# Placing the last two experts' rows with a 0/1 matrix on TensorE instead of through the table in memory

## The chip, the cores and the metric

One core of a Trainium2 chip runs the whole program. The metric is the device time of one execution in microseconds, as the median of three runs.

## The reference, cut to what matters

A sequence of 512 tokens of width 1024 goes through two blocks in f32. The first block ends with a mixture of 32 experts; each token goes to two of them. The second block begins with a final norm of the first, a norm of its own, and a product with `w_in_a_2`.

```python
expert = g_idx[:, None] * EXPERTS_PER_GROUP + top_i          # two experts per token
...
yb = (jax.nn.silu(x_blk @ w1[e]) * (x_blk @ w3[e])) @ w2[e]   # per expert, its own tokens
yb = yb * buf_w[:, None]
out = jnp.zeros((n_tok + 1, d)).at[buf_tok].add(yb)[:n_tok]   # every token sums its two rows
...
x = x + out
x = rms_norm(x, norm_final_g)                                 # "x3" before, "x4" after it
h = rmsnorm(x, ln_a); b, c, u, z = split(h @ w_in_a, 4)       # next: chunk c0 of this product
```

## The kernel before

Five engines run their own programs and meet at semaphores. The tokens lie in `x_rows`, four tiles `t` of 128 tokens by 1024 columns. PSUM has eight banks of 128 x 512 f32.

**The expert stage.** Each expert has 64 places ("slots") for its tokens; experts with more would use an overflow loop whose length `over_n` is read from memory at run time, and which doesn't run with these inputs. Per expert `e` TensorE turns the gathered rows, multiplies them with `w1` and `w3` (`hidden`, L1175: 16 matmuls, two at a time, one for output partitions 0 to 63 and one for 64 to 127), ScalarE makes the silu (L1648), VectorE the product with the other half (L2252), TensorE turns it (`turn_gated`, L1183), ScalarE copies it (L1651), and `down` (L1192) multiplies with `w2`: 8 matmuls, again two at a time, columns 0 to 511 of the result into partitions 0 to 63 of one bank and columns 512 to 1023 into partitions 64 to 127 of the same bank. An f32 matmul stands in the trace as two records, so `hidden` has 32 and `down` 16. VectorE weighs the result (`weigh`, L2255) into `y_sb`, and GpSimd scatters it by an indirect DMA into the table `y_dram` (L793), which has two half rows of 512 for each token and each of its two choices. The expert weights, 6 MB each, come over SP's queue into three slots, and SP waits for the expert three back before it loads a slot again (L653).

**Between the experts and the next product.** SP loads the raw chunk `c0` (two halves of 1 MB) once `hidden` of expert 30 is done, and `u0` after `hidden` of expert 31 (L606). When all rows are stored, SP loads eight pieces `y_back[t]` of `y_dram` (L685), for each tile one per choice, and the two gain rows `g_fin` and `g_a_row` (L688, L689). Every chunk needs a rounded high part, made by ScalarE (`high_half`, L1462), and a low part, made by VectorE (`low_half`, L2319), before TensorE multiplies in three passes (L874 to L876). VectorE then goes through a list written by hand:

- `add_back(t)` (L2325, L2326): two adds of 128 x 1024 into `x_rows`
- `scale_final(t)` (L2333): times `g_fin`
- `normalise_x4(t)` (L2339 to L2348): three small operations, a wait for ScalarE's root (L1441), a reciprocal, one 128 x 1024 product; ScalarE makes the two sums of squares for it (L1430)
- `low_x4(t)` (L2357): the low part of the turned tile; TensorE turns it (`turn_x4`, L1270) and ScalarE makes its high part (L1697)

in the order add 0, add 1, scale 0, scale 1, normalise 0, normalise 1, add 2, low 0, low 1, scale 2, add 3, normalise 2, scale 3, normalise 3, low 2, low 3. TensorE turns tiles 0 and 1, multiplies `c0` with the first 256 tokens (turning tiles 2 and 3 on the way) and then with the other 256. `spin` (L864) is dummy matmuls of 256 columns ahead of it.

Of the kernel before, what the change touches and what calls it, by code (L numbers as in the profile page):

```python
# [35 lines left out]
ALU = mybir.AluOpType  # L36
# [161 lines left out]
def second_plan():  # L198

    first = [(("x4_t", t, b), "dve") for t in range(NT) for b in range(2)]  # L200
# [7 lines left out]
    opened = closed[0:4] + [("c", j) for j in range(4)] + closed[4:8] + closed[12:]  # L208
# [87 lines left out]
def build(nc, a, out):  # L296
# [7 lines left out]
    with ctx:  # L304
# [112 lines left out]
        over_slot = w_slot[2]  # L417
        xg = [E[:, 0:512], E[:, 512:1024], B0[:, 1536:2048]]
        y_sb = [E[:, 1024:1536], E[:, 1536:2048]]
        xgT = [f3(B0, (4, 2, SLOTS), 512 * b) for b in range(2)]  # L420
# [58 lines left out]
        g_fin, g_a_row = B0[:, 0:D], B0[:, D:2 * D]  # L479
# [117 lines left out]
        def _(sp):  # L597
# [10 lines left out]
            for c in range(first_chunks):  # L608
# [4 lines left out]
                if c == 0:  # L613
                    sp.dma_start(w_gates, w_cols(w_in, 3584, 8)).then_inc(sem("w_gates_loaded"), 16)
                if c == 1:
# [48 lines left out]
            for n, c in enumerate(("c0", "u0")):  # L664
                sp.wait_ge(h_done, EXPERTS - 1 + n)
                for h in range(2):
                    load_half(2 * chunk_no[c] + h)
# [13 lines left out]
            sp.wait_ge(sem("pe_left_experts"), 1)  # L681
            for t in range(NT):
# [4 lines left out]
                if t == 1:  # L687
                    sp.dma_start(g_fin, a["norm_final_g"].partition_broadcast(P)).then_inc(sem("g_fin_loaded"), 16)  # L688
                    sp.dma_start(g_a_row, a["ln_a_2"][0].partition_broadcast(P)).then_inc(sem("g_a_row_loaded"), 16)  # L689

# [14 lines left out]
        def _(pool):  # L705
            more = sem("more_loaded2")
            pool.memset(convT[:, :, 0:CONV1 - 1], 0.0).then_inc(sem("pads_zero"), 1)
            pool.memset(mv_rows[:, :, :, P:P + 1], 1.0).then_inc(sem("pads_zero"), 1)
            loads = [(gate_b[32 * g:32 * g + HEADS, g:g + 1], a["ml_gate_b"][0, g].rearrange("(h o) -> h o", o=1))
# [106 lines left out]

            with pool.Fori(0, 4) as i:
                for n in range(6):
                    step_rows(6 * i + n, n)
            for e in range(24, EXPERTS):  # L820
                step_rows(e, e)
            for b in range(2):
                pool.wait_ge(sem(f"y_stored{b}"), 16 * EXPERTS // 2)

            n = pool.value_load(over_n, min_val=0, max_val=OVER)
            with pool.If(n > 0):
                with pool.Fori(1, OVER + 1) as k:
# [5 lines left out]
                                            y_sb[0], None, bounds_check=4 * SEQ - 1, oob_is_err=False)\  # L833
# [15 lines left out]
        def _(pe):  # L849
# [376 lines left out]

            spin(bank[0], 8)
# [28 lines left out]
            pe.nop().then_inc(sem("pe_left_experts"), 1)  # L1256


            done[0] = 0

            def turn_x4(t):

                for b in range(2):
                    o = fill(V, "x4_t", t, b)
                    if t == 0 and b == 0:
                        pe.wait_ge(sem("x3_ready"), 1)
                        spin(o, 9)
# [9 lines left out]
            spin(outs[0], 4)  # L1277
# [136 lines left out]
        def _(act):  # L1414
# [92 lines left out]
            for i in range(16 + 3):  # L1507
                if i < 16 and i % 4 == 0:
                    high_parts(("mk", "mv", "mo", "wo0")[i // 4])
                if i < 16:  # L1510
# [13 lines left out]
                    elif i >= 12:  # L1524
                        o = filled(U["proj", i])
                        act.activation(moT[:, i - 12, :], o[:, :], ACT.Copy).then_inc(done, 1)
# [126 lines left out]
            def pair(i, first=False):  # L1653
                for b in range(2):
                    e = 2 * i + b
                    act.wait_ge(h_done, e + 1)
                    if not first:
                        act.wait_ge(sem("g_ready"), e - 1)
                    silu(b).then_inc(sem("silu_e_ready"), 1)
                    act.wait_ge(g_turned, e + 1)  # L1660
                    if not first:
                        act.wait_ge(sem("y_done"), e - 1)
                    gated_cols(b).then_inc(sem("gT_ready"), 1)

            pair(0, True)
            with act.Fori(1, EXPERTS // 2) as i:
                pair(i)
            act.wait_ge(sem("y_done"), EXPERTS)
            wait_emptied(act, U["table",])
# [10 lines left out]
            high_parts("c0", "u0")  # L1680
            act.activation(root[:, 79:80], ms[:, 79:80], ACT.Sqrt)

            def square_x3(t):

                act.wait_ge(sem("x3_ready"), t + 1)
                sums(x_rows, t, 16 + t)

            def square_x3g(t):

                act.wait_ge(sem("x3g_ready"), t + 1)  # L1690
                sums_of(x3g[t], 20 + t)
# [7 lines left out]

            square_x3(0)  # L1700
            square_x3(1)
            for t in range(2):
                square_x3g(t)
                roots(16 + 2 * t, 18 + 2 * t)
            high_x4(0)
            high_x4(1)
            square_x3(2)
# [6 lines left out]
            high_x4(3)  # L1714
            for t in range(NT):
# [110 lines left out]
        def _(dve):  # L1826
# [419 lines left out]

            def rows_cols(b):
# [45 lines left out]
            pair(EXPERTS // 2 - 1, False, True)  # L2293
            step_weigh(EXPERTS // 2 - 1, 1)
            n = dve.value_load(over_n, min_val=0, max_val=OVER)
            with dve.If(n > 0):
                with dve.Fori(0, OVER) as k:
# [5 lines left out]
                    weigh(0, k + EXPERTS).then_inc(sem("y_ready"), 1)  # L2303
                    dve.wait_ge(sem("ov_stored"), 16 * k + 16)

            def low_half(name, h):

                g = 2 * chunk_no[name] + h  # L2310
                dve.wait_ge(w_high_ready, g - 1)
                lo, hi = quarter(g, False), quarter(g, True)
                if name in chunk_gain:
                    gain = chunk_gain[name]
# [252 lines left out]
```

## Time and profile before

| what | us |
|---|---|
| median of 3 runs | 1489.03 (1488.64 to 1490.09) |
| the profiled execution | 1489.01 |
| its span, first to last instruction | 1487.2 |
| TensorE busy | 1347.6 (91%) |
| VectorE busy | 536.3 (36%) |
| ScalarE busy | 414.2 (28%) |
| GpSimd busy | 391.8 (26%) |
| mean granted TensorE clock, share of full speed | 0.964 |

The expert stage lies between about 545 and 998 us; the stretch from 980 to 1043 us is where the change works. Busy time is an average over stages: only a wait that ends last in its stage sets the time.

### The profile page before, as it was taken

To read this page: it belongs to the slowest core of one execution; us is meant where nothing else is said; L and a number is where in the kernel's file an instruction comes from. 1 tells how busy PE (TensorE), PEld (TensorE's weight loads), DVE (VectorE), ACT (ScalarE), POOL (GpSimd) and SP (SyncE) were. 2 spreads that over 40 slices of the span, in tenths; PEclk is the share of its full clock that TensorE was granted. 3 is DMA by queue.
4 is the path that set the end of the run, shared out by engine and by line. 5 is a ranking of instruction groups with operands and counts; after the bars stand their busy time and mean duration, and the time that the engine had idled before them with its cause. 6 is when DMAs were issued, how large, how long until landed. Compare 5 with 4: busy or idle time off the path is not lost. (4 is left out here: it accounts for less than half of the span.)

```text
span 1487.2 us, 16780 instructions
## 1 busy us (share of the span) xinstructions
PE 1347.6 (91%) x6344; PEld 897.6 (60%) x6344; DVE 536.3 (36%) x1074; ACT 414.2 (28%) x810; POOL 391.8 (26%) x372
## 2 busy tenths in 40 slices
PE   7999998999999899988878888876999999999799
PEld 6777776898768733323323223225888887788467
DVE  3649857430242511111111111117321414563753
ACT  5333356163331100000000000014323224343641
POOL 7553223168320111111111111100444450000321
PEclk9999998999999699999999999998999999999999
DMA  7221131244205879999999999983232322222000
GB/s 209 75 97 57 58 113 64 85 164 142 85 5 213 357 297 391 418 423 422 421 423 422 422 424 421 423 339 142 85 114 85 106 93 85 85 85 85 29 22 36
DMA packets 72368, 298.27 MB, mean 201 GB/s; under 512 B 10168, under 2 KB 10216, under 8 KB 51568
## 3 DMA queue, kind: packets, MB, share of 16 engines
q1 hardware_dynamic: 64848, 282.80, 48.5%
q0 software_dynamic: 7456, 14.59, 3.0%
q8 instruction: 43, 0.70, 0.2%
q14 instruction: 21, 0.17, 0.0%
HBM read 293.16 MB, written 12.58 MB: 206 GB/s over the span
## 5 line engine op out<-in xcount | busy, mean ns | idle before, releaser
L747 POOL TENSOR_TENSOR ring_rounded<-ring,ring_rounded 128x512 fp32r<-128x512 f32 x192 | 254.1, 1362 | 348.0 <-ACT ring_rounded L1462 348.0
L874 PE MATMUL bank<-HT_rounded,ring_rounded 128*128 128x512 f32 (+1 forms) x576 | 221.2, 384 | 4.6 <-DVE ring_rounded L2357 3.5
L875 PE MATMUL bank<-ring_rounded 128*128 128x512 f32 (+1 forms) x576 | 217.6, 378 | 0.0
L876 PE MATMUL bank<-HT_rounded,ring_rounded 128*128 128x512 f32 (+1 forms) x576 | 217.6, 378 | 0.0
L1175 PE MATMUL bank<-ring,B 128*64 128x512 f32 x704 | 172.2, 639 | 43.4 <-DMA ring<-in_w 42.4
L1175 PEld LDWEIGHTS bank<-ring,B 128*64 128x64 f32 x704 | 52.6, 145 | 146.8 <-issue 106.4
L2249 DVE TENSOR_TENSOR B<-bank,small 128x512 f32<-128x512 f32 x32 | 22.1, 691 | 327.6 <-PE bank L1165 327.6
L876 PE MATMUL bank<-ring_rounded 128*128 128x512 f32 x352 | 137.7, 391 | 0.0
L1462 ACT ACTIVATE ring_rounded<-ring 128x2048 fp32r<-128x2048 f32 x54 | 102.7, 1915 | 106.1 <-DMA ring<-in_w_in_a 46.7
L874 PEld LDWEIGHTS bank<-HT_rounded,ring_rounded 128*128 128x128 f32 x576 | 108.5, 188 | 31.6 <-issue 6.2
L875 PEld LDWEIGHTS bank<-ring_rounded 128*128 128x128 f32 x576 | 108.5, 188 | 20.5 <-issue 1.0
L876 PEld LDWEIGHTS bank<-HT_rounded,ring_rounded 128*128 128x128 f32 x576 | 108.4, 188 | 20.3
L1648 ACT ACTIVATE B<-bank 64x512 f32<-64x512 f32 x32 | 18.9, 589 | 328.3 <-PE bank L1175 328.3
L874 PE MATMUL bank<-ring_rounded,XN_rounded 128*128 128x512 f32 x256 | 101.6, 397 | 1.7 <-DVE X L2409 1.5
L875 PE MATMUL bank<-ring_rounded,XN_rounded 128*128 128x512 f32 x256 | 99.7, 390 | 0.0
L1175 PE MATMUL bank<-XN,B 128*64 128x512 f32 x160 | 81.7, 665 | 18.1 <-DMA HT<-in_w 18.0
L844 POOL TENSOR_TENSOR HT<-HT,small 128x1024 f32<-128x1024 f32 (+1 forms) x16 | 26.9, 1684 | 209.8 <-DVE small L2529 209.8
L1175 PE MATMUL bank<-HT,B 128*64 128x512 f32 x160 | 81.8, 665 | 0.0
L782 POOL COPY ints<-ints 128x1 int32 x48 | 9.2, 191 | 267.1 <-DVE E L2255 265.0
L1192 PE MATMUL bank<-A,B 128*64 128x512 f32 x336 | 76.7, 598 | 0.5 <-ACT B L1651 0.5
L876 PEld LDWEIGHTS bank<-ring_rounded 128*128 128x128 f32 x352 | 66.5, 189 | 14.2
L874 PE MATMUL bank<-ring_rounded,HT_rounded 128*128 128x512 f32 x160 | 65.3, 408 | 3.5 <-DVE ring_rounded L2402 3.5
(382 smaller groups left out, 1994.5 us busy)
## 6 DMA issues: line engine op xcount, KB each, us to landing
ring<-in_w SPq DMA_DIRECT2D x88, 1024.0 KB, 30.3
A<-in_w SPq DMA_DIRECT2D x21, 2048.0 KB, 28.7
ring<-in_w SPq DMA_DIRECT2D x11, 2048.0 KB, 28.8
XN<-in_w SPq DMA_DIRECT2D x20, 1024.0 KB, 29.1
HT<-in_w SPq DMA_DIRECT2D x20, 1024.0 KB, 32.3
ring<-in_w_in_a SPq DMA_DIRECT2D x16, 1024.0 KB, 5.1
ring<-in_w_in SPq DMA_DIRECT2D x14, 1024.0 KB, 7.3
ring<-in_w_in_b SPq DMA_DIRECT2D x8, 1024.0 KB, 5.3
```

What stands on the lines that cost most here:

```text
L747: last = pool.tensor_tensor(r32(lo), lo, r32_read(quarter(g, True)[:, k, :]), ALU.subtract)
L782: pool.tensor_copy(dst, src).then_inc(written, 1)
L844: pool.tensor_tensor(S, S, rz[:, c + 4:c + 8].unsqueeze(2).to_broadcast([P, 4, n]), ALU.mult)\
L874: pe.matmul(o, r32(a_hi), r32(b_hi), start=first, stop=False)
L875: pe.matmul(o, r32(a_hi), r32(b_lo), start=False, stop=False)
L876: return pe.matmul(o, r32(a_lo), r32(b_hi), start=False, stop=last)
L1175: last = pe.matmul(bank[2 + b][64 * j:64 * j + 64, :], xgT[b][:, k, hf, :], w, start=(n == 0), stop=(n == 7), skip_group_check=True)
L1192: last = pe.matmul(bank[6 + b][64 * hf:64 * hf + 64, :], gT[b][:, k, :], w[:, k, 512 * hf:512 * hf + 512], start=(k == 0), stop=(k == 3), ...
L1462: last = act.activation(r32(hi), raw, ACT.Copy)
L1648: return act.activation(sil[b][SLOTS:P, :], bank[2 + b][0:SLOTS, :], ACT.Silu)
L2249: return dve.tensor_tensor(xgT[b], bank[b][:, :].rearrange("p (k h s) -> p k h s", k=4, h=2), g, ALU.mult)
```

## The change

- The kernel zeroes all of `y_dram` early: GpSimd clears a 128 x 512 tile `y_over`, and SP writes it out in four DMAs of 1 MB behind the fourth weight chunk. GpSimd waits for them before the experts, ScalarE before it writes `moT`, which shares the tile's memory.
- Experts 0 to 29 are scattered as before. For 30 and 31 `down_last(j, n)` puts columns 0 to 511 into bank 6 and 512 to 1023 into bank 7, both at partitions 64·j to 64·j+63, so that the two banks hold 128 slots of both experts.
- VectorE weighs bank 6 and ScalarE bank 7 into `y_last` (128 x 1024). VectorE makes, between `weigh` of expert 29 and the gate of 31, a 0/1 matrix `last_oh` (128 slots by 512 tokens).
- For each tile, `last_rows(t)` multiplies `last_oh` with `y_last` into two banks, and VectorE adds them to `x_rows` (`add_last`). For tile 1 TensorE also adds both `y_back` pieces through the identity, and VectorE's `add_back(1)` is gone.
- SP loads `y_back` once rows 0 to 29 are stored and `down_last(0)` is done, and `u0` behind it. `g_fin` and `g_a_row` move to `A1`.
- ScalarE makes `c0`'s high halves during expert 31, the first one ahead of silu 31; VectorE makes both low halves before the last weighing. `u0`'s high halves go behind `high_x4(1)` and `high_x4(3)`.
- VectorE's list is: add 0, last 0, scale 0, last 1, scale 1, normalise 0, add 2, normalise 1, low 0, last 2, last 3, low 1, scale 2, add 3, normalise 2, scale 3, normalise 3, low 2, low 3. The spins are 4 and 3 matmuls instead of 9 and 4.

```diff
+            def down_last(j, n):
+                pe.wait_ge(sem("gT_ready"), PAIR + j + 1)
+                pe.wait_ge(we_loaded[n % 3][2], 16 * ((PAIR + j) // 3 + 1))
+                pe.wait_ge(sem("y_ready"), PAIR)
...
+                for k in range(4):
+                    for hf in range(2):
+                        last = pe.matmul(bank[6 + hf][64 * j:64 * j + 64, :], gT[n % 2][:, k, :],
+                                         w[:, k, 512 * hf:512 * hf + 512], start=(k == 0), stop=(k == 3),
+                                         skip_group_check=True)
...
-            step_down(4, 6)
+            down_last(0, 6)
             step(4, 7)
-            step_down(4, 7)
+            down_last(1, 7)
             pe.wait_ge(sem("y_ready"), EXPERTS)
+            pe.wait_ge(sem("y_last_ready"), 1)
...
+            def last_rows(t):
+                for b in range(2):
+                    o = fill(V, "last", t, b)[:, :]
+                    cs = slice(512 * b, 512 * b + 512)
+                    if t == 1:
+                        pe.wait_ge(sem("y_back1"), 32)
+                        for c in range(2):
+                            pe.matmul(o, ident, y_back[t][:, c, cs], start=(c == 0), stop=False)
+                    pe.matmul(o, last_oh[:, P * t:P * t + P], y_last[:, cs], start=(t != 1), stop=True)\
+                      .then_inc(bank_filled, 1)
...
+            last_rows(0)
+            last_rows(1)
             turn_x4(0)
+            last_rows(2)
+            last_rows(3)
             turn_x4(1)
...
+            one(PAIR // 2, 0)
+            high_half("c0", 0)
+            one(PAIR // 2, 1)
+            high_half("c0", 1)
             act.wait_ge(sem("y_done"), EXPERTS)
+            act.wait_ge(sem("y_stored1"), 16 * PAIR // 2)
+            act.wait_ge(sem("last_oh_ready"), 1)
+            act.activation(y_last[:, 512:1024], bank[7][:, :], ACT.Copy, scale=last_scale)\
+               .then_inc(sem("y_last_ready"), 1)
...
+            step_gate(PAIR // 2, 1)
+            for h in range(2):
+                low_half("c0", h)
+            dve.wait_ge(sem("y_done"), EXPERTS)
...
+            dve.tensor_scalar(y_last[:, 0:512], bank[6][:, :], last_scale, None, ALU.mult).then_inc(sem("y_ready"), 2)
```

## Rows read from the trace of the kernel before

**Rows 1.** Windows (columns: stretch, length, busy time of each engine, PEclk, DMA share, GB/s)

```profile
1042.50:1487.00 444.50, 425.75 (x2096) 340.30 (x2096) 186.48 (x342) 158.90 (x339) 110.09 (x80) 1.00 0.23 76
960.00:975.00 15.00, 11.49 (x56) 4.30 (x56) 2.13 (x3) 0.90 (x2) 1.01 (x1) 1.00 1.01 425
```

**Rows 2.** Timeline of TensorE, last experts and first product (start, us, what)

```profile
980.94 3.65 PE L1192 MATMUL bank<-A,B 128*64 128x512 f32 x16 [0.47 <-ACT B L1651]
984.42 7.04 PE L1175 MATMUL bank<-ring,B 128*64 128x512 f32 x32
...
994.10 3.65 PE L1192 MATMUL bank<-ring,B 128*64 128x512 f32 x16 [0.47 <-ACT B L1651]
...
1022.86 1.89 PE L864 MATMUL bank<-cst 128*128 128x256 f32 x8
1026.65 0.39 PE L874 MATMUL bank<-HT_rounded,ring_rounded 128*128 128x256 f32 x1 [1.90 <-DVE ring_rounded L2357]
```

**Rows 3.** Timeline of VectorE, the last weighing and the list behind it

```profile
997.80 0.75 DVE L2255 TENSOR_SCALAR E<-bank,B 128x512 f32<-128x512 f32 x1 [4.20 <-PE bank L1192]
...
1009.03 1.23 DVE L2325 TENSOR_TENSOR X<-X,XN 128x1024 f32<-128x1024 f32 x1 [3.80 <-DMA XN<-y_dram]
...
1014.89 2.35 DVE L2333 TENSOR_TENSOR XN<-X,B 128x1024 f32<-128x1024 f32 x2
1017.32 0.15 DVE L2339 TENSOR_SCALAR small<-small 128x1 f32<-128x1 f32 x1
...
1019.53 0.14 DVE L2339 TENSOR_SCALAR small<-small 128x1 f32<-128x1 f32 x1
...
1024.12 2.47 DVE L2357 TENSOR_TENSOR ring_rounded<-bank,HT_rounded 128x512 fp32r<-128x512 f32 x4
```

**Rows 4.** Timelines of GpSimd and SP: scatters of experts 29 and 31, loads

```profile
981.44 0.99 POOL L793 DMA_INDIRECT y_dram<-E,ints  x1 [14.49 <-DVE E L2255]
...
999.32 0.97 POOL L793 DMA_INDIRECT y_dram<-E,ints  x1 [3.97 <-DVE E L2255]
1004.21 1.91 SPq L685 DMA_DIRECT2D XN<-y_dram  x4
```

**Rows 5.** Timeline of TensorE by record, 951 to 956 us

```profile
951.04 0.84 PE L1175 MATMUL bank<-XN,B 128*64 128x512 f32 x1 [1.92 <-DMA HT<-in_w]
...
951.68 1.06 PE L1175 MATMUL bank<-XN,B 128*64 128x512 f32 x1
...
952.53 1.06 PE L1175 MATMUL bank<-XN,B 128*64 128x512 f32 x1
...
955.34 0.59 PE L1175 MATMUL bank<-XN,B 128*64 128x512 f32 x1
955.76 0.59 PE L1175 MATMUL bank<-XN,B 128*64 128x512 f32 x1
```

**Rows 6.** Timeline of ScalarE: silu 31 and four high halves

```profile
991.50 0.59 ACT L1648 ACTIVATE B<-bank 64x512 f32<-64x512 f32 x1 [10.62 <-PE bank L1175]
...
998.80 7.31 ACT L1462 ACTIVATE ring_rounded<-ring 128x2048 fp32r<-128x2048 f32 x4 [4.75 <-issue]
```

**Rows 7.** Loads of c0's first half, issued between 975 and 976 us (L606)

```profile
L606 SPq DMA_DIRECT2D ring<-in_w_in_a x1: 390/390/390, 975.6 to 975.6; - x1
...
DMA to landing us min/median/max: 18.9/18.9/18.9
```

**Rows 8.** Lines L1256 and L2296: sequencers leaving the overflow test

```profile
L1256 PEldq EVENT_SEMAPHORE  x1: 51/51/51, 999.8 to 999.8; - x1
...
L2296 DVEq COMPARE_BRANCH  x1: 63/63/63, 998.7 to 998.7; - x1
```

**Rows 9.** Groups by shape, 480 to 520 us: an add from PSUM into X

```profile
L2081 DVE TENSOR_TENSOR X<-bank,X 128x512 f32<-128x512 f32 x1 | 0.7, 692 | 3.5 <-PE bank L876 3.5
```

**Rows 10.** Windows, columns as in Rows 1

```profile
948.00:955.00 7.00, 5.08 (x20) 2.06 (x18) 0.75 (x1) 0.38 (x1) 2.03 (x2) 0.76 1.02 424
```

**Rows 11.** Windows, columns as in Rows 1, early stage

```profile
80.00:90.00 10.00, 10.00 (x44) 7.94 (x43) 5.69 (x4) 1.79 (x3) 9.95 (x7) 1.00 0.01 2
```

More of the change, by code:

```diff
@@ L198, in second_plan @@
 def second_plan():
-    first = [(("x4_t", t, b), "dve") for t in range(NT) for b in range(2)]
+    rows = lambda name, t: [((name, t, b), "dve") for b in range(2)]
+    first = rows("last", 0) + rows("last", 1) + rows("x4_t", 0)
+    first += rows("last", 2) + rows("last", 3) + rows("x4_t", 1) + rows("x4_t", 2) + rows("x4_t", 3)
     plan = [(("c", j), "act") for j in range(4)]
@@ L689, in _ @@
                     sp.dma_start(g_a_row, a["ln_a_2"][0].partition_broadcast(P)).then_inc(sem("g_a_row_loaded"), 16)
+            sp.wait_ge(h_done, EXPERTS)
+            for h in range(2):
+                load_half(2 * chunk_no["u0"] + h)
             for c in range(chunk_no["z0"], len(chunk_list)):
@@ L1276, in _ @@
             part = chunk("c0")
-            spin(outs[0], 4)
+            spin(outs[0], 3)
             for h in range(2):
@@ L1651, in gated_cols, with one @@
                 return act.activation(gT[b], bank[4 + b][:, 0:4 * SLOTS].rearrange("p (k s) -> p k s", k=4), ACT.Copy)
[L1653 to L1667, printed above, removed]
+            def one(i, b, first=False):
+                e = 2 * i + b
+                act.wait_ge(h_done, e + 1)
+                if not first:
+                    act.wait_ge(sem("g_ready"), e - 1)
+                silu(b).then_inc(sem("silu_e_ready"), 1)
+                act.wait_ge(g_turned, e + 1)
+                if not first:
+                    act.wait_ge(sem("y_done"), e - 1)
+                gated_cols(b).then_inc(sem("gT_ready"), 1)
+            one(0, 0, True)
+            one(0, 1, True)
+            with act.Fori(1, PAIR // 2) as i:
+                one(i, 0)
+                one(i, 1)
+            one(PAIR // 2, 0)
+            high_half("c0", 0)
+            one(PAIR // 2, 1)
+            high_half("c0", 1)
             act.wait_ge(sem("y_done"), EXPERTS)
+            act.wait_ge(sem("y_stored1"), 16 * PAIR // 2)
+            act.wait_ge(sem("last_oh_ready"), 1)
+            act.activation(y_last[:, 512:1024], bank[7][:, :], ACT.Copy, scale=last_scale)\
+               .then_inc(sem("y_last_ready"), 1)
             wait_emptied(act, U["table",])
@@ L1706, in _ @@
             high_x4(1)
+            high_half("u0", 0)
             square_x3(2)
@@ L1714, in _ @@
             high_x4(3)
+            high_half("u0", 1)
             for t in range(NT):
@@ L2244, in _, with low_half @@
             wait_emptied(dve, U["table",])
+            def low_half(name, h):
+                g = 2 * chunk_no[name] + h
+                dve.wait_ge(w_high_ready, g - 1)
+                lo, hi = quarter(g, False), quarter(g, True)
+                if name in chunk_gain:
+                    gain = chunk_gain[name]
+                    for k in range(4):
+                        last = dve.scalar_tensor_tensor(r32(lo[:, k, :]), lo[:, k, :], gain[:, 4 * h + k:4 * h + k + 1],
+                                                        r32_read(hi[:, k, :]), ALU.mult, ALU.subtract)
+                else:
+                    last = dve.tensor_tensor(r32(lo), lo, r32_read(hi), ALU.subtract)
+                last.then_inc(w_split_dve, 1)
             def rows_cols(b):
```

121 lines of the change are left out of this document (77 added, 44 removed).

## The prediction

> **What bounds the kernel now.** I read the windows first. Behind 1042.5 us TensorE is busy for 425.75 of 444.5 us at full clock [rows 1]: whatever moves the end of the product with `c0` moves the end of the program by as much. In the expert stage the DMA share is 1.01 and TensorE has gaps [rows 1]: the weights set the pace there, and the change doesn't touch them. So only two questions count. When does the last expert end, and how long is the chain from there to the first product? The timelines answer both. TensorE starts `down` of expert 30 at 980.94 and from there to 997.8 it runs without a wait for a load [rows 2]; so this end is TensorE's, not the queue's. Then VectorE weighs at 997.80, GpSimd scatters at 999.32, SP loads at 1004.21, and `add_back(0)` starts at 1009.03 [rows 3, 4]: a round trip of 11.2 us. From 1009.03 VectorE works through its list almost without a pause to the end of `low_x4(1)`, 1024.12 + 2.47 = 1026.6, where TensorE starts the product at 1026.65 [rows 2, 3]. That list is the path.
>
> **Part 1, `down_last` (TensorE, on the path).** In the trace two half-width matmuls run side by side, one per half of the output partitions. At full clock each half takes a new record every 955.76 - 955.34 = 0.42 us [rows 5], call it 0.43, and yet the 32 records of `hidden` take 7.04 us, 0.22 each [rows 2]: two halves at once. The old `down` did so too: 980.94 to 984.42, 3.48 us for 16 records [rows 2]. `down_last` sends both column halves to the same partitions 64·j, so all 16 records queue on one half: 16 x 0.43 = 6.9 us, +3.4 us. This happens for expert 30 and again for 31.
>
> The Trainium skill, page "TensorEngine Tiling (Array Packing)", section "Key Properties", says that different tiles can load weights and multiply in parallel; this speaks against the change, since its pair shares one tile, and the trace agrees as far as it shows pairs on different halves overlapping.
>
> **Part 2, `c0`'s first high half ahead of silu 31 (ScalarE).** `hidden` of 31 now starts at 984.42 + 3.4 = 987.8 and ends 7.1 later, at 994.9. ScalarE is then in `high_half("c0", 0)`, which waits for a load issued at 975.6 that lands 18.9 us later, at 994.5, behind the last weights in the queue [rows 7]. One half takes 7.31 / 4 = 1.9 us [rows 6], so silu 31 starts at 996.4 and not at 994.9: +1.5 us. Behind it wait VectorE's gate 31 and TensorE's turn. `down` of 31 begins 994.10 - 991.50 = 2.6 us behind its silu [rows 2, 6]: 999.0. With 997.80 - 994.10 = 3.7 us before [rows 2, 3] and 3.4 more now, it ends at 1006.1, against 997.8: 8.3 us late. The 0/1 matrix (ten VectorE operations, the largest three of 512 columns at about 0.7 each, estimated from [rows 9]) lies between 981 and 985 under TensorE's work and costs nothing; without that cover it would be 3 to 4 us. The second high half (999.0 to 1000.9) and both low halves end before 1004, under `down_last(1)`.
>
> **Part 3, the round trip goes.** VectorE weighs at 1006.1. Its sequencer reads the overflow count meanwhile and leaves the test 1.0 us after `down` (997.8 to 998.8) [rows 3, 8], so `add_back(0)` can start at 1007.1, 2.0 us earlier than 1009.03. TensorE leaves the test 999.8 - 998.55 = 1.3 us after the weighing [rows 3, 8]; that was hidden and is now on its path: 1006.1 + 0.75 + 1.3 = 1008.1. `y_back` must be there by then. From scatter to load took 4.9 us [rows 4]; from 981.44 that gives 986.3 at the earliest. Twice that, 991, still leaves 16 us for tile 0, whose data took 4.8 us from SP's issue [rows 3, 4], plus what is left of `c0` to 997. So it is no bound.
>
> **Part 4, VectorE's new list.** A tile's two adds 2.45, scale 1.2, normalise 1019.53 - 1017.32 = 2.2, low 1.25 [rows 3]; the new `add_last` is 2 x 0.7 = 1.4 per tile [rows 9]. The new f32 matmuls cost TensorE 0.85 each (8 records of 256 columns take 1.89, so 512 columns take four such records' time, 0.9 with the tail) [rows 2].
> - add 0 to 1009.55, last 0 to 1010.95 (TensorE's two matmuls end at 1009.8), scale 0 to 1012.15.
> - last 1 waits for TensorE: eight matmuls from 1008.1 end at 1014.9, plus 0.2; its second add ends at 1015.8. Scale 1 to 1017.0.
> - normalise 0 to 1019.2, add 2 to 1021.65, normalise 1 to 1023.85. TensorE's `last_rows(2)` and `(3)`, 3.4 us behind `turn_x4(0)`, end at 1023.8, just in time.
> - low 0 to 1025.1, last 2 and 3 to 1027.9, low 1 to 1029.15.
>
> So the list is 22.1 us long where it was 17.6: four `add_last` (+5.6), one add less (-2.45), and 1.4 of waiting for tile 1. It starts 2.0 earlier and the product starts 2.5 later: 1029.2 against 1026.65. Behind it the list is the same as before, so the end of `c0` moves by 2.5 too. ScalarE's `u0` halves (1.9 each) fit its gaps; without them the next square would wait at most 1.9.
>
> **Part 5, the early zeroing.** Four stores of 1 MB behind the fourth chunk. The queue carries nothing from 80 to 90 us [rows 11]; at the 425 GB/s of [rows 1] 4 MB need 10 us. TensorE is busy throughout and does not wait for loads there, so I take 0. The nearest bounds: 0, and 10 us of queue time of which a part could show if stores were half as fast; below zero nothing, since no work goes away there.
>
> **Part 6, the clock.** Behind the 1.92 us gap at 951.04 the records come 0.85 us apart instead of 0.43 [rows 5]: 1.2 GHz in place of 2.4, for four pairs, until about 954.3; the window shows 0.76 [rows 10]. That costs 4 x 0.43 = 1.7 us wherever TensorE is the path. The loop's other gaps, 3.5 us in 15 together, left 1.00 [rows 1]. The changed stretch has gaps of 2.9 us (994.9 to 997.8, silu), 2.0 (1006.1 to 1008.1), 2.4 (ahead of `turn_x4(0)`), and 1.2 (1.9 before) ahead of the product. Behind the first stands `down_last(1)`, behind the second the matmuls that VectorE waits for, behind the last the product; each slow spell there costs 0 to 1.7. Bounds 0 and 5.1; I take one in full, because the first gap is longer than the one that did it.
>
> **Sum.** Against the profiled execution's 1489.0 (span 1487.2 and 1.8 around it; equal to the median): +3.4 +1.5 +3.4 for the late end of `down`, -10.2 for the removed trip (11.2 less the 1.0 of the overflow test; with the 8.3 before it this is the -2.0 of part 3 to within rounding), +4.5 for the list, +1.7 for one slow spell: +4.2, **1493.2 us**.
>
> **Rivals.** This kernel can be told from no change at about 0.2%, 3.0 us.
> - A, no slow spell: all else as above, +2.5, 1491.5, within 0.2%. For it: gaps of 1.7 to 1.9 were passed at full clock. If the `c0` half also lands 1.5 us earlier, 1490.0. Together 0.31.
> - B, forecast, one spell, 1493.2: 0.36.
> - C, two or three spells, or a dip at the product's start that also delays tiles 2 and 3: +5.9 to +7.6, 1494.9 to 1496.6: 0.17.
> - D, the other side: the pair in `down_last` overlaps after all although it shares its output half, because the two banks and not the half let records run together. Then `hidden` 31 ends at 991.5, but silu 31 still waits for ScalarE until 996.4 (the load lands at 994.5), so `down` ends at 996.4 + 2.6 + 3.7 = 1002.7, 3.4 earlier than in my sum: 1489.8 with a slow spell, 1488.1 without. If the load is early too, another 4.9 goes: 1483.2, faster than before. It decides from 16 records in less than about 4 us. 0.06, half of it under 1486.
> - E, the list shrinks: VectorE starts `add_back(0)` early and ScalarE's and TensorE's steps hide more than I count; -3 us or more against A, 1486: 0.06.
> - F, the change doesn't work as told: an overflow pass, or zeroes that come too late and hold GpSimd. The test was left at once [rows 8] and the stores are 450 us ahead: 0.04, either above 1497 or at no difference.
>
> **Chances.** Slower by over 0.2% (above 1492.0): B, C, half of F and none of A: 0.55. Within: A, part of D: 0.34. Faster: the rest of D and E, 0.11. The range of 8 in 10 leaves out E with the best of D, and the far end of C and F: 1488.0 to 1496.5.
>
> **What would show it.** `down_last`'s 16 records in 6.9 us for both experts (step 1; under 4 is D). Silu 31 about 1.5 us behind the end of `hidden` 31, with ScalarE's L1462 line just ahead (step 2). From the last weighing to `add_back(0)` under 0.5 us (step 3). VectorE waiting about 1.4 us for the second bank of tile 1, and 22 us from the first add to the end of `low_x4(1)` (step 4). No wait of TensorE for loads between 80 and 130 us (step 5). Granted clock of 0.5 somewhere between 996 and 1030 us (step 6). The prediction is wrong if the expert stage itself ends at another time, since its pace is the queue's, or if TensorE's last 440 us are no longer free of gaps.

## The result, and the profile after

| what | before | after |
|---|---|---|
| median, us | 1489.03 (1487.07 to 1491.67, 5 runs) | 1496.16 (1494.62 to 1502.16, 5 runs) |
| the profiled execution | 1489.01 | 1499.28 |
| its span | 1487.2 | 1497.2 |
| mean granted TensorE clock | 0.964 | 0.961 |

Timed against each other the ratio is 1.0055, 95% interval 1.0035 to 1.0075: the change makes the kernel slower by 8.2 us (5.2 to 11.2). Two later measurements of the same kernel, below, gave 1.0031 and 1.0044, so 4.6 and 6.6 us. The forecast was 4.2 us slower, a ratio of 1.0028: below the first interval, but inside those of both repeats. That the forecast was too small is shown by the profile's marks below and not by the times alone.

The first lines of the page of the changed kernel:

```profile
span 1497.2 us, 16827 instructions
PE 1369.7 (91%) x6356; PEld 902.2 (60%) x6356; DVE 541.4 (36%) x1089; ACT 414.6 (28%) x811; POOL 388.3 (26%) x371
HBM read 293.16 MB, written 16.25 MB: 207 GB/s over the span
```

TensorE is busy for 22.1 us more than before's 1347.6, and 3.7 MB more are written to memory (12.58 before), the zeroes less two experts' rows. The timeline of TensorE through the changed stretch (start, us, engine, line, operation; in brackets the idle time before it and what ended it):

```profile
982.10 6.65 PE L1254 MATMUL bank<-A,B 128*64 128x512 f32 x15 [0.47 <-ACT B L1699]
...
988.59 0.59 PE L1254 MATMUL bank<-A,B 128*64 128x512 f32 x1
988.65 7.40 PE L1194 MATMUL bank<-ring,B 128*64 128x512 f32 x31
999.20 0.71 PE L1202 MATMUL bank<-cst,B 64*128 64x64 f32 x4 [3.15 <-DVE B L2331]
1000.38 9.74 PE L1254 MATMUL bank<-ring,B 128*64 128x512 f32 x16 [0.47 <-ACT B L1699]
1012.14 3.36 PE L1302 MATMUL bank<-E,B 128*128 128x512 f32 x4 [2.02 <-issue]
...
1025.30 1.23 PE L1313 MATMUL bank<-cst,XN 128*128 128x128 f32 x8 [2.59 <-DVE XN L2451]
1026.32 5.27 PE L1302 MATMUL bank<-E,B 128*128 128x512 f32 x8
...
1034.80 0.39 PE L893 MATMUL bank<-HT_rounded,ring_rounded 128*128 128x256 f32 x1 [0.66 <-DVE ring_rounded L2460]
```

It answers to [rows 2]. `down_last(0)` (L1254 at 982.10) takes 6.5 us to its last record where `down` took 3.5, and `hidden` 31 (L1194) ends at 988.65 + 7.40 = 996.05, 13.95 us behind the start of `down` 30 and not 10.5. `down_last(1)` takes 9.74 us for the same 16 records, and the first product starts 52.7 us behind `down` 30, where it was 1026.65 - 980.94 = 45.7.

ScalarE around silu 31 (L1696), which answers to [rows 6]:

```profile
995.80 1.91 ACT L1509 ACTIVATE ring_rounded<-ring 128x2048 fp32r<-128x2048 f32 x1 [13.76 <-DMA ring<-in_w_in_a]
997.74 0.59 ACT L1696 ACTIVATE B<-bank 64x512 f32<-64x512 f32 x1
```

The high half waits 13.76 us for `c0`'s load, and silu 31 waits behind it until 997.74, 1.7 us after its input is there. VectorE from the last weighing, which answers to [rows 3]:

```profile
1010.22 0.75 DVE L2397 TENSOR_SCALAR E<-bank,B 128x512 f32<-128x512 f32 x1 [5.77 <-PE bank L1254]
1011.37 1.23 DVE L2416 TENSOR_TENSOR X<-X,XN 128x1024 f32<-128x1024 f32 x1 [0.40 <-issue]
...
1015.54 0.69 DVE L2428 TENSOR_TENSOR X<-bank,X 128x512 f32<-128x512 f32 x1 [0.94 <-PE bank L1302]
...
1018.44 0.69 DVE L2428 TENSOR_TENSOR X<-bank,X 128x512 f32<-128x512 f32 x1 [0.87 <-PE bank L1302]
1021.01 0.69 DVE L2428 TENSOR_TENSOR X<-bank,X 128x512 f32<-128x512 f32 x1 [1.88 <-PE bank L1302]
...
1033.47 1.28 DVE L2460 TENSOR_TENSOR ring_rounded<-bank,HT_rounded 128x512 fp32r<-128x512 f32 x2
```

The round trip is gone: 1.15 us from the last weighing to the first add instead of 11.2. But the last weighing is 28.1 us behind `down` 30 instead of 16.9, and the list lasts from 1011.37 to 1034.75, 23.4 us instead of 17.6; VectorE waits three times for TensorE's banks in it, 3.7 us together.

The windows of the same kernel (stretch, length, busy time of each engine, granted clock, DMA share, GB/s) tell why TensorE is late:

```profile
999.00:1000.00 1.00, 0.71 (x4) 0.55 (x4) 0.97 (x2) 0.06 (x1) 0.00 (x0) 0.50 1.04 350
1004.00:1005.00 1.00, 1.00 (x3) 0.31 (x2) 0.45 (x1) 0.00 (x0) 0.00 (x0) 0.50 1.06 404
1006.00:1007.00 1.00, 1.00 (x4) 0.32 (x3) 0.00 (x0) 0.00 (x0) 0.00 (x0) 1.00 1.05 387
1013.00:1014.00 1.00, 1.00 (x2) 0.41 (x2) 0.95 (x2) 0.00 (x0) 0.00 (x0) 0.50 0.52 190
1017.00:1018.00 1.00, 1.00 (x4) 0.52 (x3) 0.56 (x1) 0.82 (x3) 0.00 (x0) 1.00 0.00 0
1027.00:1029.00 2.00, 2.00 (x4) 0.79 (x3) 1.59 (x6) 0.76 (x3) 0.00 (x0) 0.50 0.00 0
1042.50:1497.00 454.50, 437.16 (x2152) 349.30 (x2150) 191.19 (x352) 164.78 (x347) 109.96 (x80) 0.98 0.22 75
```

The granted clock is 0.50, so 1.2 GHz, from 999, near the end of TensorE's gap of 3.15 us (996.05 to 999.20), to between 1005 and 1006; again from 1013 to about 1016, behind the gap of 2.02; and a third time around 1027 to 1029, behind the gap of 2.59. Below, such a stretch at 1.2 GHz is called a spell. Behind 1042.5 it is 0.98 where [rows 1] had 1.00.

### The profile page after: what moved, and what is told of

Read it like the earlier page. It is cut to its first block and busy times, and to the rows that moved or that the text cites. A ratio compares the mean times of both kernels' runs of the same rounds, so it can differ in the third digit from the quotient of the medians.

```text
span 1497.2 us, 16827 instructions
## 1 busy us (share of the span) xinstructions
PE 1369.7 (91%) x6356; PEld 902.2 (60%) x6356; DVE 541.4 (36%) x1089; ACT 414.6 (28%) x811; POOL 388.3 (26%) x371
## 5 line engine op out<-in xcount | busy, mean ns | idle before, releaser
L1194 PE MATMUL bank<-ring,B 128*64 128x512 f32 x704 | 180.4, 663 | 35.9 <-DMA ring<-in_w 35.0
L1194 PEld LDWEIGHTS bank<-ring,B 128*64 128x64 f32 x704 | 55.2, 151 | 144.4 <-issue 111.7
L2328 DVE TENSOR_TENSOR B<-bank,small 128x512 f32<-128x512 f32 x32 | 22.1, 692 | 326.7 <-PE bank L1184 326.7
L1696 ACT ACTIVATE B<-bank 64x512 f32<-64x512 f32 x32 | 18.9, 589 | 314.9 <-PE bank L1194 314.9
L1194 PE MATMUL bank<-XN,B 128*64 128x512 f32 x160 | 74.0, 609 | 26.1 <-DMA HT<-in_w 26.1
L1194 PE MATMUL bank<-HT,B 128*64 128x512 f32 x160 | 74.1, 610 | 0.0
L1211 PE MATMUL bank<-A,B 128*64 128x512 f32 x320 | 73.1, 598 | 0.0
## 6 DMA issues: line engine op xcount, KB each, us to landing
A<-in_w SPq DMA_DIRECT2D x21, 2048.0 KB, 28.9
```

The costliest lines, as they stand in the source:

```text
L1194: last = pe.matmul(bank[2 + b][64 * j:64 * j + 64, :], xgT[b][:, k, hf, :], w, start=(n == 0), stop=(n == 7), skip_group_check=True)
L1211: last = pe.matmul(bank[6 + b][64 * hf:64 * hf + 64, :], gT[b][:, k, :], w[:, k, 512 * hf:512 * hf + 512], start=(k == 0), stop=(k == 3), ...
L1696: return act.activation(sil[b][SLOTS:P, :], bank[2 + b][0:SLOTS, :], ACT.Silu)
L2328: return dve.tensor_tensor(xgT[b], bank[b][:, :].rearrange("p (k h s) -> p k h s", k=4, h=2), g, ALU.mult)
```

## The experiments

Where nothing else is said, "before" and "after" in a label's text are the kernels before and after the change. Every kernel here computes the whole reference. Each has two readings. The first is its ratio to the kernel before, from 11 or 12 timed executions against some 35 (the first, of the row "after", 5 against 5). The second is its profile, by five marks behind the start of `down` of expert 30 (between the profiles of one kernel they agree to 0.2 us):

| kernel | silu 31 | down 31 | last weighing | first add | product | ratio (95%) |
|---|---|---|---|---|---|---|
| before | 10.6 | 13.2 | 16.9 | 28.1 | 45.7 | 1 |
| after | 15.6 | 18.3 | 28.1 | 29.3 | 52.7 | 1.0055 (1.0035 to 1.0075) |
| x0_after | 15.6 | 18.3 | 28.2 | 29.4 | 52.8 | 1.0031 (1.0008 to 1.0053) |
| x10_after | 15.7 | 18.3 | 28.1 | 29.3 | 52.7 | 1.0044 (1.0025 to 1.0063) |
| x1_zero | 10.6 | 13.2 | 18.5 | 28.9 | 46.4 | 1.0007 (0.9989 to 1.0024) |
| x11_zero | 10.6 | 13.2 | 18.6 | 28.8 | 46.2 | 0.9998 (0.9981 to 1.0015) |
| x2_serial | 12.3 | 14.9 | 21.8 | 31.6 | 48.6 | 1.0022 (1.0005 to 1.0040) |
| x3_overlap | 15.6 | 18.3 | 23.6 | 24.7 | 47.5 | 1.0027 (1.0008 to 1.0046) |
| x4_silu | 14.0 | 16.6 | 23.8 | 24.9 | 46.6 | 1.0030 (1.0013 to 1.0047) |
| x5_both | 10.6 | 13.2 | 20.7 | 21.3 | 47.3 | 1.0008 (0.9989 to 1.0027) |
| x6_spin | 15.6 | 18.2 | 25.4 | 26.5 | 48.4 | 1.0026 (1.0007 to 1.0044) |
| x7_all | 10.6 | 13.1 | 20.7 | 21.3 | 46.6 | 0.9998 (0.9975 to 1.0021) |
| x8_low | 10.6 | 13.2 | 18.6 | 19.7 | 44.6 | 0.9993 (0.9971 to 1.0014) |
| x9_full | 10.6 | 13.1 | 16.8 | 19.0 | 44.0 | 0.9986 (0.9965 to 1.0006) |

The theory when they were planned: the file in `down_last`, the order on ScalarE and slow spells of the clock make the loss, the zeroing does not. The rivals: the zeroing delays the early stage or the experts; or the loss lies behind the product and not in the stretch.

### The change again, as it is (x0_after, x10_after)

No edit.

> The changed kernel as it is, timed again beside the others. All theories: 1.003 to 1.007 of the kernel before (+5 to +10 us). In the profile: the 16 records of each last down take 6.9 us at full clock and more where the clock is low; silu 31 starts right behind ScalarE's first high half of c0; VectorE's list from the first add to the end of low 1 takes 22 to 24 us.

> The changed kernel once more, beside the two versions of it in the same runs: 1.003 to 1.0055 of the kernel before, as the two series so far gave. The product at 50 to 53 us from the start of down 30, by how many slow spells fall on the stretch.

Medians 1494.46 against 1488.14, and 1495.52 against 1489.02: 6.3 and 6.5 us; by the ratios 4.6 (1.2 to 7.9) and 6.6 (3.7 to 9.4). The marks repeat the first profile to 0.1 us although `down` 30 starts at 985.1 and 975.1 in these two and at 982.1 in the first. So the 7.0 us of the stretch are the change's, slow spells included. The start of `down` 30, which moves by 10 us between profiles of the same program, is not; that it was 1.2 us later in the first profile than before's 980.94 says nothing.

### The early zeroing alone (x1_zero, x11_zero)

```diff
+                if c == 3:
+                    sp.wait_ge(sem("zeros_ready"), 1)
+                    for q in range(4):
+                        sp.dma_start(y_dram[SEQ * q:SEQ * q + SEQ, :]..., y_over...).then_inc(sem("y_zeroed"), 16)
...
+            pool.memset(y_over, 0.0).then_inc(sem("zeros_ready"), 1)
...
+            pool.wait_ge(sem("y_zeroed"), 16 * 4)
```

> The kernel before with only the early zeroing added (four stores of 1 MB and the waits for them). Theory T (the loss lies in the stretch from expert 30 to the first product): within 1 us of before. Rival Z (in the changed kernel's trace SP loads the first expert's weights at 462.87 us against 457.70, so the stores delay the mixing part): +1 to +5 us, and that load again late.

> The kernel before with only the early zeroing, once more, since the first series left 0 to +3.6 us open. Theory T: within 1 us of before. Rival Z: +1.5 to +3.5 us, with the start of down 30 later than without it.

Medians 1489.78 and 1489.18, intervals on both sides of 1: no difference that can be measured (at most 3.6 and 2.2 us by the intervals), and the rival of the zeroing falls. Its second sign did come: SP loads the first expert's weights at 462.64 and 462.01 us, 457.70 before. But `down` 30 starts at 981.34 and 980.29, 980.94 before, so the delay doesn't reach the experts' end; and x10_after, which zeroes too, loads at 456.73. The profile gave something else. The last `down` of x1_zero, in before's order and behind the same gap as in before:

```profile
993.36 0.66 PE L1191 MATMUL bank<-cst,B 64*128 64x64 f32 x4 [1.50 <-DVE B L2261]
994.50 5.35 PE L1200 MATMUL bank<-ring,B 128*64 128x512 f32 x16 [0.47 <-ACT B L1660]
```

Before took 3.65 us for these 16 records, behind a gap of the same length. So the length of the gap just ahead does not decide alone; a kernel that has such gaps can land at either level.

### One half after the other in the kernel before (x2_serial)

```diff
+            def down_serial(b, slot):
+                w = as_expert(slot[2], 2).rearrange("p (k n) -> p k n", k=4)
+                for hf in range(2):
+                    for k in range(4):
+                        last = pe.matmul(bank[6 + b][64 * hf:64 * hf + 64, :], gT[b][:, k, :], ...)
...
+                run = down_serial if isinstance(e, int) and e >= EXPERTS - 2 else down
```

> The kernel before, where only the down products of experts 30 and 31 issue the four matmuls of one output half and then the four of the other, so that no two records of a pair stand on different halves. Same data, same places. Theory T: 16 records take 6.9 us instead of 3.5, twice: +6.8 us. Rival K (TensorE's order hardly matters, the low clock made the loss): under +2 us.

The edit was meant to keep every record of one half behind those of the other. It doesn't do that, and the rows show it. TensorE, then windows (the first two of L1202 alone; their columns are stretch, length, PE, weight loads, granted clock, DMA share, GB/s):

```profile
981.85 4.13 PE L1202 MATMUL bank<-A,B 128*64 128x512 f32 x13 [0.47 <-ACT B L1662]
985.40 0.64 PE L1175 MATMUL bank<-ring,B 128*64 128x512 f32 x1
...
996.77 6.85 PE L1202 MATMUL bank<-ring,B 128*64 128x512 f32 x16 [0.47 <-ACT B L1662]
```

```profile
981.85:983.60 1.75, 1.75 (x4) 0.60 (x5) 1.00 1.01 414
983.60:985.35 1.75, 1.75 (x9) 0.72 (x8) 1.00 0.95 392
```

```profile
997.00:998.00 1.00, 1.00 (x2) 0.28 (x2) 0.00 (x0) 0.00 (x0) 0.95 (x1) 0.50 1.07 410
1000.00:1001.00 1.00, 1.00 (x7) 0.53 (x7) 0.00 (x0) 0.00 (x0) 0.00 (x0) 1.00 1.05 389
```

In `down` 30 four records run alone for 1.75 us, and then the records of the second half come beside those of the first (9 in the next 1.75 us), although eight stand ahead of them in the program. So the second half starts 1.8 us late and not 3.5, `hidden` 31 follows each half as it comes free (its first record at 985.40), and silu 31 is 1.7 late (12.3 instead of 10.6). In `down` 31 the halves overlap in the same way (7 records in 1000 to 1001), but its first three records stand in a spell (0.50 in 997 to 998). Its 6.85 us are therefore an overlapped product at a low clock. That they equal the 6.9 of the forecast is chance, and this run doesn't test what it was built for.

6.8 us were expected; the last weighing is 4.9 late, the round trip takes 9.8 us here and 11.2 before, the list waits 0.7 less for `y_back`, and 2.9 are left at the product (3.2 timed). What one half costs is read from the changed kernel: there all 16 records of a `down_last` go to the same 64 partitions, with banks 6 and 7 in turn, and at full clock they take 7.08 us (x4_silu and x6_spin), where the split halves of x5_both take 3.65. For expert 30 this shows in full in silu 31: 14.0 in x4_silu, where it waits for nothing else, against 10.6.

The Trainium skill, page "TensorEngine Tiling (Array Packing)", section "Key Properties", lets different tiles of the array work in parallel. These rows agree: 7 records stand in 1 us at full clock where both halves have work.

### Both downs side by side in the changed kernel (x3_overlap)

```diff
-                for k in range(4):
-                    for hf in range(2):
-                        last = pe.matmul(bank[6 + hf][64 * j:64 * j + 64, :], gT[n % 2][:, k, :], ...)
+                down(n % 2, w_slot[n % 3]).then_inc(y_done, 1)
...
-                    pe.matmul(o, last_oh[:, P * t:P * t + P], y_last[:, cs], start=(t != 1), stop=True)
+                for e in range(2):
+                    for b, o in enumerate(outs):
+                        r = slice(64 * b, 64 * b + 64)
+                        last = pe.matmul(o, last_ohs[e][r, P * t:P * t + P], y_last[r, 512 * e:512 * e + 512], ...)
```

Each expert has its own bank, with the column halves at partitions 0 to 63 and 64 to 127 as before; each column half of a tile then takes two matmuls over 64 slots instead of one over 128.

> The changed kernel, where only the placing of the last two downs is changed: each fills its own bank with both halves side by side as before the change, and last_rows uses four matmuls of 64 rows per tile, two at a time, in place of two of 128 rows (VectorE makes two 0/1 matrices). Theory T: down 30 gives back 3.4 us but silu 31 still waits for c0's half, down 31 gives back 3.4: -5.0 us and some of the low clock against the changed kernel (silu at about the same time, so -3.4 at the least). Rival K: under 2 us.

```profile
983.42 3.65 PE L1212 MATMUL bank<-A,B 128*64 128x512 f32 x16 [0.47 <-ACT B L1698]
986.91 7.04 PE L1195 MATMUL bank<-ring,B 128*64 128x512 f32 x32
1000.50 0.71 PE L1203 MATMUL bank<-cst,B 64*128 64x64 f32 x4 [6.55 <-DVE B L2330]
1001.68 5.22 PE L1212 MATMUL bank<-ring,B 128*64 128x512 f32 x16 [0.47 <-ACT B L1698]
```

The downs are short again. Of the 3.4 us won at expert 30 nothing arrives: silu 31 still starts at 15.6, since `c0`'s load lands when it lands and ScalarE waits for it first. What was 3.15 us of idle TensorE is now 6.55. The file and the order on ScalarE hide each other at this place, and `down` 31 is slow here too (5.22, not 3.65). Stretch 47.5, ratio 1.0027.

### Silu 31 ahead of the high halves (x4_silu)

```diff
-            high_half("c0", 0)
             one(PAIR // 2, 1)
+            high_half("c0", 0)
             high_half("c0", 1)
```

> The changed kernel, where only ScalarE's order is changed: both high halves of c0 come behind silu 31 and its copy, as in no case to hold them up. Times below are from the start of down 30 to the start of the first product: 45.7 us before, 52.7 and 52.8 in two profiles of the changed kernel. Theory T: silu 31 at 13.9 us in place of 15.6, the product at 51 us, and up to 2 us less where the shorter gap spares TensorE a slow spell during down 31; -2 to -4 us. Rival K (only the clock matters): the same 52.7 unless the clock is full.

```profile
997.54 0.66 PE L1202 MATMUL bank<-cst,B 64*128 64x64 f32 x4 [1.51 <-DVE B L2331]
998.68 7.08 PE L1254 MATMUL bank<-ring,B 128*64 128x512 f32 x16 [0.47 <-ACT B L1699]
1007.77 1.98 PE L1302 MATMUL bank<-E,B 128*128 128x512 f32 x4 [2.01 <-issue]
```

Silu 31 comes 1.6 us earlier, as part 2 has it, and the last weighing 4.3: the other 2.7 is `down_last(1)`, 7.08 us at full clock instead of 9.74. The list takes 21.7 us (1007.02 to 1028.72), not 23.4. The gap ahead of `last_rows(0)` is as long as in the changed kernel (2.01), yet its four records take 1.98 us, at full clock, and not 3.36. In the profile these few moved lines give back 6.1 of 7.0 us (2 to 4 were expected). The timed ratio, 1.0030, gives back less. The profile is one execution without these two spells; that other executions of x4_silu had them would explain it, but no row shows it.

### Dummy matmuls in the gaps (x6_spin)

```diff
+                if isinstance(e, int) and e == EXPERTS - 1:
+                    spin(bank[0], 5)
                 pe.wait_ge(sem("g_ready"), e + 1)
...
             down_last(1, 7)
+            spin(bank[0], 4)
...
-                        spin(o, 4)
+                        spin(o, 9)
```

> The changed kernel, where only dummy matmuls are added in TensorE's idle stretches: 5 behind hidden 31, 4 behind down 31, 9 in place of 4 ahead of the first turn. None of them should make anyone wait. Theory T: the granted clock stays 1.00 from down 31 to the product; down 31 takes 6.9 us in place of 9.7 and the last rows of tile 1 come 1.8 earlier: the product at 48 to 49 us from the start of down 30 in place of 52.7, -4 us. Rival S (the spells come from elsewhere, so that dummy work doesn't prevent them): 52.7 stays.

This is the test that tells the clock from the waits: no wait goes, only TensorE's idle time in them. TensorE and the windows:

```profile
990.37 2.42 PE L883 MATMUL bank<-cst 128*128 128x256 f32 x10
993.50 0.69 PE L1202 MATMUL bank<-cst,B 64*128 64x64 f32 x4 [0.71 <-DVE B L2334]
994.67 7.08 PE L1256 MATMUL bank<-ring,B 128*64 128x512 f32 x16 [0.47 <-ACT B L1702]
...
1003.90 1.98 PE L1305 MATMUL bank<-E,B 128*128 128x512 f32 x4 [0.23 <-issue]
```

```profile
994.00:1004.00 10.00, 9.30 (x27) 3.70 (x26) 5.82 (x4) 4.15 (x4) 0.00 (x0) 1.00 1.04 389
1004.00:1018.00 14.00, 13.57 (x46) 8.04 (x47) 11.00 (x17) 4.79 (x11) 0.00 (x0) 1.00 0.31 115
```

The gaps of 3.15, 2.02 and 2.59 shrink to 0.71, 0.23 and 0.43, the clock is 1.00 throughout, silu 31 and `down` 31 stay where they were (15.6, 18.2), and the product starts at 48.4 instead of 52.7, inside the 48 to 49 expected. So 4.3 us of the 7.0 are the clock, and filling the gaps gives them back. Which gap brings on which spell doesn't follow, since all three were filled at once: in x4_silu the first alone was shorter, and neither of the first two spells came. The remaining 2.7 are the waits and the longer list. The ratio, 1.0026, is not told apart from the changed kernel's 1.0031 to 1.0055: the gain is seen in one profile's marks only.

### Both mended, and what then became late (x5_both, x7_all)

x5_both is x3_overlap and x4_silu together. x7_all adds spins of 2, 3 and 9, and the overflow count read ahead of the last `down` and the last weighing.

> Both at once: downs with their halves side by side, and ScalarE's high halves behind silu 31. Theory T: silu 31 at 10.6 us and the last weighing at 16.9 us from the start of down 30, as in the kernel before; then 1.0 for the overflow test and the list of 22 to 23 us: the product starts at 40 to 42 us, 4 to 5 us earlier than before, so the time is 2 to 5 us under the kernel before (the early stores may take 1 back). Rival Z (the early stores or the longer list eat it): not under before.

```profile
998.15 3.65 PE L1212 MATMUL bank<-ring,B 128*64 128x512 f32 x16 [0.47 <-ACT B L1698]
1007.60 3.79 PE L1299 MATMUL bank<-E,B 64*128 64x512 f32 x8 [5.80 <-issue]
```

```profile
1000.63 2.29 DVE L2322 TENSOR_TENSOR ring_rounded<-ring,ring_rounded 128x2048 fp32r<-128x2048 f32 x1 [3.76 <-ACT ring_rounded L1508]
1003.33 2.29 DVE L2322 TENSOR_TENSOR ring_rounded<-ring,ring_rounded 128x2048 fp32r<-128x2048 f32 x1 [0.41 <-ACT ring_rounded L1508]
1005.66 0.75 DVE L2399 TENSOR_SCALAR E<-bank,B 128x512 f32<-128x512 f32 x1
```

The product was expected at 40 to 42 and comes at 47.3. `down` 31 starts at 13.2 and is over after 3.65 us, exactly as before. The last weighing is still 3.8 us late (20.7): `c0`'s two low halves (L2322) stand ahead of it in VectorE's program, and they wait for ScalarE, which waits for the load. TensorE idles 5.80 us, and tile 0's eight records then take 3.79 us where x3_overlap had 1.99. In the kernel before those low halves lay in the round trip, where they cost nothing.

> Downs side by side, high halves behind silu 31, dummy matmuls (2, 3 and 9), and the overflow count read by TensorE and VectorE before the last down and the last weighing. Theory T: the product starts at 38 to 40 us from the start of down 30, 6 to 8 us earlier than before; 1481 to 1484 us. Rival Z: gains of the stretch are lost elsewhere, and the time stays at or above 1487.

```profile
997.20 3.78 PE L1302 MATMUL bank<-E,B 64*128 64x512 f32 x8 [3.49 <-DVE E L2403]
```

The last weighing is at 20.7 again, though `down` 31 runs at full clock (3.65 us): the split of `c0` holds it and not the clock. Behind `down` 31 the dummy matmuls fill the wait only in part. A gap of 3.49 us is left, and tile 0's eight records take 3.78 us, at 1.2 GHz. Stretch 46.6 where 38 to 40 was expected, ratio 0.9998 where 1481 to 1484 us was. One of its 12 executions took 3504 us and the others at most 1493.43; the ratio leaves that one out, and no row shows what held it.

### The low halves into the list (x8_low, x9_full)

```diff
             step_gate(PAIR // 2, 1)
-            for h in range(2):
-                low_half("c0", h)
...
-            for step, t in ((add_back, 0), (add_last, 0), (scale_final, 0), (add_last, 1), ...
+            for step, t in ((add_back, 0), (add_last, 0), (scale_final, 0), (low_c0, 0), (add_last, 1), ...
+                            (low_x4, 0), (low_c0, 1), (add_last, 2), ...
```

x8_low is x5_both with this, and with VectorE weighing both banks, that of expert 30 while `hidden` 31 runs (ScalarE weighed bank 7). x9_full adds spins (2, 3 and 6) and the early read of the count.

> Times from the start of down 30. In the profile of the kernel with downs side by side and silu 31 first, down 31 ended at 17 us, but VectorE weighed only at 20.7: c0's low halves stood ahead of the weighing and waited for ScalarE's high halves and these for the load. Here VectorE weighs 30 during hidden 31 and 31 at once, and the two low halves stand in its list (behind scale 0 and behind low 0). Nothing else differs. Theory L (c0's split had been hidden by the removed round trip and became the new wait): the weighing back at 16.9 us, the first add at 18, TensorE idle 2 us instead of 5.8, so fewer slow spells; the product at 42 to 44 us against 47.3, 2 to 4 us earlier than before the change. Rival M (the split only moves: 4.6 us of low halves in the list cost what they gave): 46 to 48 us as it is.

```profile
1000.18 0.75 DVE L2395 TENSOR_SCALAR E<-bank,B 128x512 f32<-128x512 f32 x1 [6.68 <-PE bank L1212]
1001.33 1.23 DVE L2415 TENSOR_TENSOR X<-X,XN 128x1024 f32<-128x1024 f32 x1 [0.39 <-issue]
...
1006.72 2.29 DVE L2317 TENSOR_TENSOR ring_rounded<-ring,ring_rounded 128x2048 fp32r<-128x2048 f32 x1
```

The last weighing now waits for TensorE alone, the first add is 8.4 us earlier than before (19.7 against 28.1), and the product 1.1 (44.6; 42 to 44 was expected): the two low halves (the first of them at 1006.72) and the four `add_last` are in the list. The remaining slow `down` (5.35 us, as in x1_zero) is the clock (0.50 in 996 to 998).

> The same with dummy matmuls (2 behind hidden 31, 3 behind down 31, 6 ahead of the first turn) and the overflow count read before the last down and the last weighing. Theory L: the product at 40 to 42 us from the start of down 30; 3 to 5 us under the kernel before. Rival M: 46 us and no difference.

`down` 31 takes 3.65 us and the last weighing is back at 16.8. The first add is at 19.0 (it waits 1.49 us for `y_back`), the list takes 24.9 us, and the product starts at 44.0, 1.7 us earlier than before; 40 to 42 was expected. One spell is left, over the last dummy matmuls and the product's first records, behind a gap of 3.58 us:

```profile
1025.80 2.74 PE L884 MATMUL bank<-cst 128*128 128x256 f32 x6 [3.58 <-DVE X L2430]
```

Median 1487.99 against 1489.02, ratio 0.9986 with an interval that reaches 1.0006: the best of all versions, but not told apart from the kernel before.

## Why the prediction was right or wrong, point by point

The direction was right and the time, 1496.2, lies inside the range; the size was 4.2 forecast against 8.2 measured (4.6 and 6.6 by the ratios of the repeats).

- **Part 1, `down_last`: right.** 6.5 us to its last record for expert 30, 7.08 with its tail for expert 31 at full clock (x4_silu, x6_spin), +3.4 each. Rival D, that the two banks let the records run together, is out: these 16 records alternate between banks 6 and 7 and still come one by one, while the old `down` has both halves in one bank and takes 3.65.
- **Part 2, silu 31: right.** 1.5 forecast, 1.6 measured by x4_silu. 2.6 us from silu to `down` 31, as forecast.
- **Part 3, the trip: right.** From the last weighing to the first add 1.15 us in place of 11.2, and TensorE leaves the test 2.02 us behind `down`, where 2.0 was forecast.
- **Part 4, the list: right at full clock.** 22.1 forecast, 21.7 in x4_silu and 21.8 in x6_spin. The waits for banks were put at 1.4; at full clock they are 2.1 and 2.25, which shorter steps elsewhere in the list make up for, partly luck. In the changed kernel the list is 23.4 and the waits 3.7; those 1.6 more are the clock again. Without a spell the forecast had the product 2.5 us late; x6_spin has 48.4 - 45.7 = 2.7.
- **Part 5, the zeroing: right.** No difference in two measurements.
- **Part 6, the clock: this step failed.** One spell of 1.7 us was taken, and two on the path cost 4.3. Its number and its price were both too small. The number: three of the four gaps named are followed by 0.50; the forecast counted the first alone, because its 2.9 us are longer than the 1.92 ahead of the spell in [rows 5]. By that same row its gaps of 2.0 and 2.4 were longer too, and the forecast gave no reason to pass over them. Why the gap of 2.02 had a spell here and that of 2.01 in x4_silu had none stays open. Two spells lie on the path; the third, over `last_rows(2)` and `(3)`, delays nothing, since VectorE's adds at 1031.08 wait for nothing. The price: 1.7 was four side-by-side pairs of [rows 5]. The spell over `down_last(1)` lasts from 1000.4 to between 1005 and 1006, its records come one by one at double their time, and it costs 9.74 - 7.08 = 2.7. The second costs 1.6 of list (23.4 - 21.8). Rival C, two or three spells, 5.9 to 7.6 us in the stretch, is what happened: 7.0.

So in the stretch: forecast 2.5 + 1.7 = 4.2, measured 2.7 + 4.3 = 7.0.

**The other 3.3 us of the profiled execution.** 1499.28 - 1489.01 is 10.3. 1.2 is the start of `down` 30, which is scatter. 0.3 lies around the span (2.1 instead of 1.8). 1.9 lies behind the start of the product (462.4 instead of 460.5), where the forecast had nothing. It goes with the granted clock of the late stage (us from the start of the product to the end, and the clock in 1240 to 1310, 1350 to 1400 and 1400 to 1450 us; all from windows):

```
after, x0_after, x10_after   462.3 to 462.5   0.95 0.97 0.93
x1_zero, x11_zero            462.2 to 462.4   0.95 0.97 0.93
x6_spin                      461.1            0.98 0.97 0.93
before                       460.5            0.98 1.00 1.00
x2_serial                    460.6            0.98 1.00 0.97
x4_silu, x8_low              459.9, 460.5     0.98 1.00 1.00
x7_all                       458.8            1.00 0.97 1.00
x3_overlap, x5_both, x9_full 458.9 to 459.2   1.00 1.00 1.00
```

Two kernels with nothing in common but the zeroing share the worst of it, and the mended ones, which zero as well, don't have it. x1_zero's and x11_zero's medians are those of before, so the profile's 1.9 is not proof of a cost in the timed runs either. Why a stage that the change doesn't touch gets its slow spells in one kernel and not in another stays open; no run here separates it.

**Where the 10 us of the removed trip went.** By x9_full, where both late ends are mended and no spell stands ahead of the product's last dummy matmuls: the first add comes 9.0 us earlier than before, and the list is 7.3 longer (24.9 against 17.6), of which 4.6 are `c0`'s low halves (2 x 2.28) that the trip used to hide. A second such cover went in the changed kernel, whose ScalarE had to make `c0`'s high half ahead of silu 31.

Another order of `hidden` 31's records would not win back `down_last(0)`'s 3.4 us, by an estimate from these rows: its first record on the other half already starts at 988.17, ahead of `down_last(0)`'s last at 988.59, and the 16 records that it has for partitions 0 to 63 need 16 x 0.43 = 6.9 us from 988.59 + 0.43 = 989.0 on, to 995.9, whatever their order. It ends at 996.05.

## What to carry to other kernels

A wait of 11 us is worth its length only after everything that lay under it has been given another place: list what other engines did meanwhile, and ask for each piece where it stands when the wait is gone and whose program it then blocks. Give two half-width matmuls that should run together different output partitions. When a change opens gaps on TensorE ahead of a chain that sets the time, price a slow spell behind each of them with the records that stand there, one by one or in pairs, and try a few dummy matmuls in the gap first.

## What the runs showed of the hardware that was not expected

- Gaps of 3.15 and 2.02 us ahead of `down_last(1)` and `last_rows(0)` went with 1.2 GHz in all three profiles of the changed kernel (the marks agree to 0.1 us). Filled to 0.71 and 0.23 us, the clock stayed at 2.4 GHz. The length of a gap doesn't decide alone. One of about 2.0 ahead of `last_rows(0)` was followed by full clock in x4_silu (2.01), x3_overlap (2.03) and x8_low (1.97). One of 1.50 (with 0.47 behind the turn) was followed by full clock in before, x4_silu and x5_both, and by a slow `down` in x1_zero, x11_zero and x8_low (5.35 us each) and in x2_serial (0.50 in 997 to 998).
- An f32 matmul of 512 columns with 64 output partitions can start beside the records of another that uses the other 64, even of another product (985.40 in x2_serial) and ahead of records that stand before it in the program: in x2_serial the second half of `down` 30 starts after four of the first half's eight records, 1.75 us in.
- The same stage of 440 us behind the product, with the same instructions, took 458.8 to 462.5 us by how many spells at 1.2 GHz fell in it, and the experts' end moved by 10 us between profiles of one kernel (975.1 to 985.1). Single executions of this kernel can't tell 3 us; marks inside the stretch can.
